# Key selection that keeps all its counts, and another order of loads, stores and bias work in the stick-breaking stage

## The reference

```python
def stick_breaking(q, k, v, q_pos, k_pos):          # 6 heads x 64
    z = jnp.einsum('bqhd,bkhd->bhqk', q, k) * HEAD_DIM ** -0.5
    causal = (k_pos[None, :] < q_pos[:, None])[None, None]
    log_keep = jnp.where(causal, jax.nn.log_sigmoid(-z), 0.0)
    after = lax.cumsum(log_keep, axis=3, reverse=True) - log_keep
    a = jnp.where(causal, jnp.exp(jax.nn.log_sigmoid(z) + after), 0.0)
    return jnp.einsum('bhqk,bkhd->bqhd', a, v)

def dsa_attend(q, qi, wi, q_pos, k, v, ki, k_pos, topk):   # topk = 256
    score = jnp.einsum('bqhk,bqh->bqk', jax.nn.relu(jnp.einsum('bqhe,bke->bqhk', qi, ki)), wi)
    score = jnp.where(admissible[None], score, -jnp.inf)
    _, idx = lax.top_k(score, topk)                 # then attention over the chosen keys
```

## Time and profile before

| | |
|---|---|
| median of three runs (lowest, highest) | 4870.93 us (4870.72, 4872.74) |
| the profiled execution: its time; its span | 4873.81 us; 4872.1 us |
| mean granted TensorE clock | 0.975 |
| busy over the span: PE, DVE, ACT, POOL | 4540.9, 3541.8, 1625.3, 1345.9 us |
| projection and selection, first layer | 435.5 to 1270.4 us |
| stick stage, first layer; second layer | 1270.4 to 1608.9 us; from 3703.2 us |

### The profile page before, as it was taken

The page is one execution under the profiler, slowest core; times in us unless marked ns, Lnnn a source line. Parts: engine busy times, 40 slices in busy tenths (PEclk is TensorE's granted clock), DMA queues, the critical chain, the costliest instruction groups (busy, mean ns, idle before and its releaser), DMA issues. The chain is left out here.

```text
span 4872.1 us, 71199 instructions
## 1 busy us (share of the span) xinstructions
PE 4540.9 (93%) x25390; PEld 2608.6 (54%) x25390; DVE 3541.8 (73%) x5925; ACT 1625.3 (33%) x2410; POOL 1345.9 (28%) x1329
## 2 busy tenths in 40 slices
PE   8988999999699998899989889999996999988999
PEld 6423445744376666564464234457444666665643
DVE  2786999999889653554527869999998896535545
ACT  3552101100366665330035521011003666653300
POOL 3310146200111797110033101462001117971100
PEclk9999999999899999999999999999998999999999
DMA  2102111211311002885211021112113110028842
GB/s 77 33 16 71 49 23 37 76 57 62 111 53 55 23 27 81 268 271 171 97 46 32 16 71 49 22 40 75 59 61 109 55 53 23 27 87 272 271 136 91
DMA packets 343730, 396.44 MB, mean 81 GB/s; under 512 B 100311, under 2 KB 264242, under 8 KB 340050
## 3 DMA queue, kind: packets, MB, share of 16 engines
q1 hardware_dynamic: 318034, 375.10, 24.7%
q10 hardware_dynamic: 25344, 16.79, 1.3%
HBM read 297.71 MB, written 94.14 MB: 80 GB/s over the span
## 5 line engine op out<-in xcount | busy, mean ns | idle before, releaser
L976 DVE TENSOR_SCALAR_CACHE_REDUCE arena<-arena 128x384 uint8<-128x384 f32 (+14 forms) x960 | 1405.2, 1534 | 6.9 <-DVE arena L1014 0.5
L850 PE MATMUL banks<-arena 128*128 128x512 f32 x2176 | 937.4, 592 | 0.0
L850 PEld LDWEIGHTS banks<-arena 128*128 128x128 f32 x2176 | 409.9, 189 | 520.4 <-issue 520.4
L853 PE MATMUL banks<-arena 128*128 128x384 f32 (+1 forms) x2048 | 620.3, 459 | 2.9 <-POOLq L144 2.9
L1488 POOL TENSOR_SCALAR arena<-arena 128x128 f32<-128x128 f32 (+15 forms) x192 | 578.3, 3026 | 59.9 <-DVE arena L1514 57.2
L1289 DVE TENSOR_TENSOR_SCAN arena<-arena 128x129 f32<-128x129 f32 (+3 forms) x480 | 508.0, 1109 | 72.3 <-ACT arena L1209 58.5
L853 PEld LDWEIGHTS banks<-arena 128*128 128x128 f32 x2048 | 379.9, 189 | 208.4 <-issue 4.2
L450 DVE SCALAR_TENSOR_TENSOR arena<-arena 128x512 f32<-128x512 f32 (+3 forms) x532 | 403.5, 758 | 118.3 <-ACT arena L418 69.2
L2013 PE MATMUL banks<-arena 128*128 128x512 f32 x1024 | 445.0, 597 | 13.3 <-DMA arena<-in_w_out 13.3
L1503 DVE CUSTOM_DVE_ANT_0 arena<-banks,arena 128x512 f32<-128x512 f32 (+3 forms) x480 | 269.6, 607 | 237.0 <-PE banks L1414 236.8
L357 PE MATMUL banks<-arena 64*128 64x512 f32 (+3 forms) x1216 | 308.4, 594 | 60.9 <-ACT arena L418 59.6
(11 more groups left out here) (200 smaller groups left out, 5558.9 us busy)
## 6 DMA issues: line engine op xcount, KB each, us to landing
arena<-in_cache_sb_kv SPq DMA_DIRECT2D x256, 384.0 KB, 4.3
arena<-in_cache_dsa_kv SPq DMA_DIRECT2D x144, 128.0 KB, 4.3
arena<-in_x_prompt SPq DMA_DIRECT2D x32, 512.0 KB, 4.1
arena<-mixT SPq DMA_DIRECT2D x32, 512.0 KB, 4.0
arena<-xs SPq DMA_DIRECT2D x32, 512.0 KB, 4.4
arena<-in_cache_dsa_kv ACTq DMA_DIRECT2D x112, 128.0 KB, 4.5
arena<-in_w_in SPq DMA_DIRECT2D x8, 1536.0 KB, 7.6
out<-arena SPq DMA_DIRECT2D x64, 192.0 KB, 1.9
```

The costliest lines, as they stand in the source:

```text
L850: m = nc.tensor.matmul(bank[i % 4][:, :], W2[c % 2][:, k, j * P:(j + 1) * P], xT[:, k, t * FREE:(t + 1) * FREE], start=(k == 0), stop=(k = ...
L853: m = nc.tensor.matmul(bank[i % 4][:, 0:WD[name]], xT[:, k, t * P:(t + 1) * P], W2[c % 2][:, k, 0:WD[name]], start=(k == 0), stop=(k == KC ...
L976: nc.vector.tensor_scalar(out[0:r, 0:v.shape[-1]], v, thr[0:r, t:t + 1], 0.0, ALU.is_ge, ALU.add, accum_out=cnt[0:r, t:t + 1]).then_inc(s_ ...
```

## The change

There are four parts, the same in both layers.

1. The selection keeps the counts of all 32 passes in a table `history` (32x17 values a partition, in the words that the running count `cum` uses later). The per-pass work is `flip` and one instruction that makes the next threshold from the last one. Behind the passes, one instruction over 544 values and one `reduce_max` give `above`.
2. The barriers lose the two increments of the semaphore `wait_passed`.
3. In the stick stage SP no longer issues the 48 bias stores and the second pair's loads ahead of the first store of `byo`: six bias stores go behind each of the first eight `byo` stores, and the loads of the next pair (and of the next stage) are spread behind them.
4. The 14 prompt tiles of `bias_end` leave DVE. POOL does them in 38 pieces of up to 512 columns, two behind the mask of each of 19 query tiles: t = 12 to 15 of the first pair, 4 to 15 of the second, 4 to 6 of the third.

```diff
         def barrier(eng, n):
-            eng.sem_inc(s_near, 1)
             eng.drain().then_inc(s_bar, 1)
             eng.wait_ge(s_bar, 5 * (n + 1))
-            eng.sem_inc(s_near, 1)
...
+        NPASS = 32
+        history = cum_words[:, 0:17 * NPASS].rearrange("p (k t) -> p k t", k=NPASS)
...
+            def counts(k):
+                for j, t in enumerate(SELTILES):
+                    v = scores(t)
+                    dve.wait_ge(s_cnt, at(s_cnt, n + NSEL * k + j - 1))
+                    nc.vector.tensor_scalar(dummy[j % 2][:, 0:v.shape[-1]], v, thr[:, t:t + 1], 0.0,
+                                            ALU.is_ge, ALU.add, accum_out=history[:, k, t:t + 1]).then_inc(s_cnt, 1)
+                dve.wait_ge(s_cnt, at(s_cnt, n + NSEL * (k + 1)))
...
-                nc.vector.scalar_tensor_tensor(low, cnt, TOPK - 0.5, cnt, ALU.is_lt, ALU.mult).then_inc(s_rej, 1)
-                nc.vector.tensor_scalar(flip, cnt, TOPK - 0.5, float(1 << b), ALU.is_ge, ALU.mult).then_inc(s_bit, 1)
-                dve.wait_ge(s_rej, at(s_rej, r0 + 4 + 2 * k))
-                nc.vector.tensor_tensor(above, above, low, ALU.max).then_inc(s_rej, 1)
-                dve.wait_ge(s_bit, at(s_bit, b0 + 5 + 3 * k))
+                nc.vector.tensor_scalar(flip, history[:, k + 1, :], TOPK - 0.5, float(1 << b), ALU.is_lt, ALU.mult).then_inc(s_bit, 1)
+                dve.wait_ge(s_bit, at(s_bit, b0 + 5 + 2 * k))
                 if b:
-                    nc.vector.scalar_tensor_tensor(thr.bitcast(I32), flip, 1 << (b - 1), fbits, ALU.bitwise_xor,
+                    nc.vector.scalar_tensor_tensor(thr.bitcast(I32), flip, 1 << (b - 1), thr.bitcast(I32), ALU.bitwise_xor,
                                                    ALU.bitwise_xor).then_inc(s_bit, 1)
-                    nc.vector.tensor_tensor(fbits, fbits, flip, ALU.bitwise_xor).then_inc(s_bit, 1)
...
+            nc.vector.scalar_tensor_tensor(history, history, TOPK - 0.5, history, ALU.is_lt, ALU.mult).then_inc(s_rej, 1)
+            dve.wait_ge(s_rej, at(s_rej, r0 + 1))
+            nc.vector.reduce_max(above, history.rearrange("p k t -> p t k"), AX_X).then_inc(s_rej, 1)
...
-            for b in range(NB):
...
-            load_stick_qk(sp, l, 1)
-            load_stick_values(sp, l, 1, 0, NT, s_bvl[1])
-            load_gate(1)
...
                 sp.dma_start(YTD[256 + p * P:256 + (p + 1) * P, q * FREE:(q + 1) * FREE], byo[g % 2]).then_inc(s_bys[g % 2], 16)
+                if g < NB:
+                    store_bias(g)
+                if g == 0:
+                    load_stick_qk(sp, l, 1)
+                if g == 1:
+                    load_stick_values(sp, l, 1, 0, NT, s_bvl[1])
+                if g == 2:
+                    load_gate(1)
...
+        BPIECES = [(SC_OFF[t] + a, min(SC_OFF[t] + a + FREE, SC_OFF[t + 1])) for t in SELTILES[0:NSEL - 1] for a in range(0, (t + 1) * P, FREE)]
+        BAFTER = [n for n in range(NSU) if n >= 24 and diagonal(n) and SUNITS[n][1] >= 4][0:len(BPIECES) * 2]
...
+                    for k in range(2 if n in BAFTER else 0):
+                        if done < len(BPIECES):
+                            v = sc[:, BPIECES[done][0]:BPIECES[done][1]]
+                            nc.gpsimd.tensor_scalar(v, v, 1.0, -OUT_OF_REACH, ALU.subtract, ALU.mult)
+                            done += 1
...
-                if n % 8 == 4 and n // 8 < NSEL - 1:
-                    bias_end(SELTILES[n // 8])
```

More of the change, by code:

```diff
@@ L131, in carver @@
             return carve
-        s_bar, s_near = raw_sem("barrier"), raw_sem("wait_passed")
+        s_bar = raw_sem("barrier")
         def at(s, count):
@@ L209, in build @@
         sc, scs, sel_state = scores_region(carve)
-        fbits, flip = (sel_state[:, 17 * k:17 * k + 17].bitcast(I32) for k in range(2))
-        thr, cnt, need, above, low = (sel_state[:, 17 * k:17 * k + 17] for k in range(2, 7))
+        flip = sel_state[:, 0:17].bitcast(I32)
+        thr, need, above = (sel_state[:, 17 * k:17 * k + 17] for k in range(1, 4))
         xn = [arena[:, SCW + D * v:SCW + D * v + D] for v in range(2)]
@@ L969, in project_gpsimd @@
                         n += 1
-        def count(dve, t, n, out):
-            r, v = P, scores(t)
-            dve.wait_ge(s_cnt, at(s_cnt, n - 1))
-            nc.vector.tensor_scalar(out[0:r, 0:v.shape[-1]], v, thr[0:r, t:t + 1], 0.0,
-                                    ALU.is_ge, ALU.add, accum_out=cnt[0:r, t:t + 1]).then_inc(s_cnt, 1)
-        NCOUNT = (NBIT + 1) * NSEL
-        NSTEP = 3 + 3 * NBIT
-        s_rej = sem("rejected_counts")
-        def select_vector(dve, l):
-            b0, n, r0 = l * NSTEP, l * NCOUNT, l * (2 * NBIT + 3)
-            nc.vector.memset(cnt, 0.0).then_inc(s_bit, 1)
+        NCOUNT = NPASS * NSEL
@@ new lines, in build @@
+        NSTEP = 4 + 2 * NBIT
+        s_rej = sem("refused_counts")
+        def select_vector(dve, l):
+            b0, n, r0 = l * NSTEP, l * NCOUNT, 2 * l
+            def counts(k):
[5 more added lines that the diff above has]
+                dve.wait_ge(s_cnt, at(s_cnt, n + NSEL * (k + 1)))
+            nc.vector.memset(cum_words[:, 0:17 * NPASS], 0.0).then_inc(s_bit, 1)
@@ L986, in select_vector @@
             nc.vector.memset(thr, 0.0).then_inc(s_bit, 1)
-            nc.vector.memset(above, 0.0).then_inc(s_rej, 1)
             dve.wait_ge(s_bit, at(s_bit, b0 + 2))
-            for j, t in enumerate(SELTILES):
-                count(dve, t, n + j, dummy[j % 2])
-            dve.wait_ge(s_cnt, at(s_cnt, n + NSEL))
-            nc.vector.scalar_tensor_tensor(low, cnt, TOPK - 0.5, cnt, ALU.is_lt, ALU.mult).then_inc(s_rej, 1)
-            nc.vector.tensor_scalar(fbits, cnt, TOPK - 0.5, -1.0, ALU.is_lt, ALU.mult).then_inc(s_bit, 1)
@@ L994, in select_vector @@
-            dve.wait_ge(s_rej, at(s_rej, r0 + 2))
-            nc.vector.tensor_tensor(above, above, low, ALU.max).then_inc(s_rej, 1)
+            counts(0)
+            nc.vector.tensor_scalar(flip, history[:, 0, :], TOPK - 0.5, -1.0, ALU.is_lt, ALU.mult).then_inc(s_bit, 1)
             dve.wait_ge(s_bit, at(s_bit, b0 + 3))
-            nc.vector.tensor_scalar(thr.bitcast(I32), fbits, 1 << 30, None, ALU.bitwise_xor).then_inc(s_bit, 1)
+            nc.vector.tensor_scalar(thr.bitcast(I32), flip, 1 << 30, None, ALU.bitwise_xor).then_inc(s_bit, 1)
@@ L998, in select_vector @@
             for k in range(NBIT):
                 b = NBIT - 1 - k
-                n += NSEL
-                dve.wait_ge(s_bit, at(s_bit, b0 + 4 + 3 * k))
-                for j, t in enumerate(SELTILES):
-                    count(dve, t, n + j, dummy[j % 2])
-                dve.wait_ge(s_cnt, at(s_cnt, n + NSEL))
-                dve.wait_ge(s_rej, at(s_rej, r0 + 3 + 2 * k))
-                nc.vector.scalar_tensor_tensor(low, cnt, TOPK - 0.5, cnt, ALU.is_lt, ALU.mult).then_inc(s_rej, 1)
@@ L1015, in select_vector @@
-                    dve.wait_ge(s_bit, at(s_bit, b0 + 7 + 3 * k))
-                else:
-                    nc.vector.tensor_tensor(thr.bitcast(I32), fbits, flip, ALU.bitwise_xor).then_inc(s_bit, 1)
-                    dve.wait_ge(s_bit, at(s_bit, b0 + 6 + 3 * k))
+                else:
+                    nc.vector.tensor_tensor(thr.bitcast(I32), thr.bitcast(I32), flip, ALU.bitwise_xor).then_inc(s_bit, 1)
+            dve.wait_ge(s_bit, at(s_bit, b0 + 4 + 2 * NBIT))
             b = l * NSTAT
-            dve.wait_ge(s_rej, at(s_rej, r0 + 3 + 2 * NBIT))
+            nc.vector.scalar_tensor_tensor(history, history, TOPK - 0.5, history, ALU.is_lt, ALU.mult).then_inc(s_rej, 1)
@@ L1107, in stick_sync, with store_bias @@
             load_gate(0)
[L1108 to L1109 removed]
+            sp.wait_ge(s_bias, at(s_bias, l + 1))
+            def store_bias(b):
                 a = 32 * (b // 2) + b % 2
@@ L1123, in stick_sync @@
                     load_stick_qk(sp, l, 2)
+                if g == 4:
                     load_stick_values(sp, l, 2, 0, NT, s_bvl[0])
+                if g == 5:
                     load_gate(2)
```

12 lines of the change are left out of this document (9 added, 3 removed).

## The result

The changed kernel takes 4842.6 us (median of 5 runs, 4840.6 to 4846.3), the kernel before 4870.7 in the same comparison: a ratio of 0.9949, 95% interval 0.9938 to 0.996. The forecast was 4842.

What follows compares the result with a forecast made beforehand. DVE's selection bounds its stage, and a DVE wait for a `byo` store leaves a hole in the stick stage. -15 - 1 - 23 + 10 = -29 from 4873.8 gives 4845, 4842 us as median; range 4830 to 4854.

Steps and rivals of the forecast that it cites:

- Selection, -15: Key selection on DVE: shorter passes less the added work behind them save 7.4 us a layer, 15 us in two layers.
- Barriers, -1: At the 14 barriers, dropping the increments saves 0.7 us, taken as 1 us, at most 4.8.
- SP's order, -23: Stick stage: DVE's wait for a `byo` store goes, worth 12.7 and 10.6 us in the two layers.
- nothing new is late: Stick stage: a moved store may come 5 us late, but its buffer is wanted only four tiles after its turn.
- the hole moves: Stick stage: DVE waits at a later `byo` store, half of the 23 us remain, 4854 to 4860; chance 0.07.
- Bias off DVE, 0: Stick stage: taking the 14 bias instructions off DVE gains 0, at best 2 us a layer.
- Bias on POOL, +10: Stick stage: 38 pieces on POOL delay DVE's scans by 0.4 us each in dense tiles, 5 us a layer.
- Late masks: Stick stage: POOL's masks queue behind two pieces and DVE's scans wait, +10 a layer, 4862 us; chance 0.15.
- The lock: Stick stage: pieces keep DVE's scans out throughout, 27 to 30 us a layer in place of 5, 4892; chance 0.12.
- Clearing DVE pays: Stick stage follows DVE's total more: 4 us a layer come on top and pieces fall into waits, 4826; chance 0.13.
- the gate's wait gone: Sign in the stick stage: DVE's wait for `mixT<-arena`, 13.40 us and 11.33 in the second layer, disappears.
- The scans in tiles 4 to 7: Sign in the second pair: scans 0.4 us longer where a piece lies under them; 1.4 longer would mean a rival holds.

Runs made afterwards that it cites:

- the last experiment: The changed kernel with one more two-input instruction of 17 elements, not waited for, in each of 31 selection bit steps: 4840.0 us, ratio 0.9939.
- whole tiles: The changed kernel with each tile's bias as one GpSimd instruction (14 of 384 to 2048 columns) in place of 38 pieces: 4883.2 us, ratio 1.0028.

## Why the prediction was right

The time came out as forecast, but the terms did not each come out. Against the sum on record:

**Selection, -15: about -11 (9.4 us with the selection alone).** The table was sized rightly: 0.51, 0.73 and 1.10 us make the 2.3 of the forecast. The quiet step was also right, 0.42 for the 0.44 taken. What failed is the sentence that 0.06 + 0.04 + 0.04 us of excess belong to the three two-input instructions, so that one of them would keep 0.05. The excess over the median was 0.146 a step before and is 0.142 now, with one such instruction in place of four; it is 0.165 with the selection alone. It falls due in a few steps (17 of 62 now, all but one beside an instruction of POOL), on whichever instruction stands there, `flip` among them, which has one input; the one extra two-input instruction of the last experiment added none. The steps meet other instructions of POOL in each kernel, so that the two totals agree this closely is partly chance. So a step went from 0.81 to 0.565, not 0.49, and 31 steps gave 7.7 us and not 9.6: 5 to 6 net a layer where 7.4 were forecast, in the lower part of the range of 8 to 22 for both.

**Barriers, -1: about -2.5.** The increments are 0.24 of the 0.34 us passage, not a seventh, and the eleven barriers that can be read add up to 2.5 us. The times alone (ratio 0.9996) could not have told.

**SP's order, -23: -22.4.** Both the size (12.7 and 10.6 forecast, 11.3 and 11.1 found by the order alone) and "nothing new is late" held. In the changed kernel DVE waits for no store of `byo` in either stick stage. The rival in which the hole moves is out.

**Bias off DVE, 0: about -2 a layer.** At best 2 us a layer was the forecast's own bound. It is worked out from two kernels (with the bias on DVE and with none): 1.8 us in the second and third pair. The waits of the earlier trace rows took the small instructions for the most part, not wholly. As the forecast had it, the differences' block moved from the bias instruction to the next scan and gave nothing.

**Bias on POOL, +10: about +5.** The size was off by two: a piece of 512 makes the scans it meets 0.23 us longer on average, not 0.4, and DVE's 6.9 us of extra busy time cost the stage 2.3 and 2.9 us. The mechanism was right for pieces of this size: in the earlier trace rows the first 0.62 us at most were open to a hold, and no scan was found more than 0.54 longer with a piece of 512. The forecast did not foresee the step beyond 1024 columns; the change stays below it. These two terms together were forecast at +5 a layer and are within 1 us of 0, as the kernel with the bias alone (1.0003) and the kernel with the bias back show.

**The hit itself is in part luck.** The errors of the terms cancel only in part: 4 us too much gain in selection, 9 too much cost in the bias, 1.5 too little at the barriers. By the terms as measured, -11 - 22.4 + 1 - 2.5, the kernel should be 35 us faster. The spans differ by 32.3, the medians by 28.1, and the interval of the ratio says 20 to 30. So the terms as measured would have missed by 7 us the time that the forecast hit within 1. Some 3 us of this are the wait under the lower clock at the start of the first pair, which the profile of the changed kernel has in both layers and that of before in neither. What else lies between is within the spread of stages that no edit touches, and stays open.

**The rivals.** *Late masks:* the changed kernel has no wait of DVE for POOL's masks in either layer, and none with whole tiles. *The lock:* with pieces of up to 1024 columns it does not hold scans out throughout; with 1152 and more a scan waits 3.6 to 4.2 us, and the kernel is slower than before, on the side where the forecast had put this rival. The Trainium skill's page "SBUF — State Buffer" (section "Who interferes with whom") has GpSimd and a two-input DVE instruction exclude each other for the whole instruction. For one-input pieces up to 1024 columns the traces differ (a piece of 512 takes 2.46 us and delays by 0.23), and the measurement decides; for longer ones they lie nearer to it, though there too the hold ends before the piece does. *Clearing DVE pays:* by its 2 us a layer, which the pieces take back. *The hole moves:* no, see SP's order above.

**What was to be seen.** Right: PE's wait at 17 (16 and 15 forecast), the gate's wait gone, no mask wait. The stick stage was forecast at 331 and is 328.7. Too hopeful: selection's stage 7 us sooner (6.0 and 5.0), the step at 0.5 (0.565). The scans in tiles 4 to 7 are longer by less than the 0.4 named.

## What to carry to other kernels

Take from a row's mean what lies over its quiet value before you multiply it: here the time lost to another engine's work fell due where the two met, and removing three of five instructions there removed none of it (0.146 us a step before, 0.142 and 0.165 after). An instruction that nothing near waits for was free here in the gap in which its neighbour waits for a semaphore, so count the waits of a short chain and not its instructions. When work is moved to GpSimd beside a busy VectorE, cut it (here at 1024 columns or less), and look also for what GpSimd already does beside it: the largest further gain found in this stage was in four subtractions that it does, each of which holds VectorE up for longer than VectorE needs to do it.

## What the runs showed of the hardware

- A one-input instruction of GpSimd on up to 1024 fp32 columns made the scans it met longer by 0.95 us at most, and was itself stretched (512 columns: 1.57 in the selection stage, 2.46 on average beside scans). In the selection stage it held a small instruction of VectorE that met its start so that this one ended 0.71 us after that start, in eight meetings of eight, and did not hold those that came 0.62 us or later. From 1152 to 2048 columns it made one scan 3.6 to 4.2 us longer, hardly more for 2048 than for 1152. Why there is a step between 1024 and 1152 was not found out.
- A subtraction on 2048 columns takes GpSimd 4.5 to 5.4 us in these traces and holds a scan of VectorE for some 4.2 of them; VectorE does it in 2.27. Whether halves of 1024 columns would hold less was not tried.
- In a chain of two small VectorE instructions with a wait between them the second starts 0.21 us after the first. A third that neither of them waits for fits in between at no cost.
- Two semaphore increments by each engine, one ahead of a barrier's drain and one behind its wait, cost 0.24 us of a passage of 0.34.
- At the start of the stick stage TensorE's granted clock was at 0.69 or at 1.00 in the same 5 us of work, from run to run and layer to layer, and the lower went with one wait of VectorE for ScalarE of 1.2 to 1.4 us.
